# A transformer block's routing stage on one Trainium2 core: the picks in one comparison, the tokens formed in two halves later, a register load moved

## The reference, cut to what matters

```python
def moe(h, w_router, b_router, w_gate, b_gate, w_up, b_up, w_down, b_down):
    logits = h @ w_router + b_router
    top_logit, top_idx = lax.top_k(logits, TOP_K)      # 4 of 32 experts
    gates = jax.nn.softmax(top_logit, axis=-1)
    ...
        g = jnp.minimum(xb @ w_gate[e] + b_gate[e], 7.0)
        u = jnp.clip(xb @ w_up[e] + b_up[e], -7.0, 7.0)
        act = g * jax.nn.sigmoid(1.702 * g) * (u + 1)
        return act @ w_down[e] + b_down[e]
```

## Time and profile before

| | |
|---|---|
| median of 3 runs | 1881.03 us (1880.22 to 1882.22) |
| the profiled execution: its own time | 1879.11 us |
| its span, first to last instruction | 1877.3 us |
| mean granted TensorE clock | 0.996 |
| PE busy / DVE busy / ACT busy | 1824.7 / 505.1 / 348.3 us |
| router, from the scaled logits to the end of the block | 208.9 to about 221.6 us |
| experts' block, first gather to the last matmul of w_down | 221.9 to 1140.8 us |

### The profile page before, as it was taken

One profiled execution on the slowest core, in us unless ns is written; L12 is line 12 of the kernel. 1 busy time (PEld: TensorE's weight loads), 2 busy tenths in 40 slices (PEclk: granted clock), 3 DMA queues, 4 the chain that ended last, 5 costly groups with the idle time before them and its releaser, 6 DMA issues. The chain is left out here.

```text
span 1877.3 us, 21793 instructions
## 1 busy us (share of the span) xinstructions
PE 1824.7 (97%) x8661; PEld 998.6 (53%) x8662; DVE 505.1 (27%) x1093; ACT 348.3 (19%) x688; POOL 10.9 (1%) x14
## 2 busy tenths in 40 slices
PE   6999899999999999999999999999999999999998
PEld 5757533333333333333333336768885466788743
DVE  1754411111011111011111104542025443211355
ACT  3221411111111111111111113332000032220001
POOL 0000000000000000000000000000000000000001
PEclk9999899999999999999999999999999999999999
DMA  9986599999999999999999999423355443134252
GB/s 401 324 184 276 207 416 430 431 432 432 431 431 431 433 431 431 431 431 432 431 431 430 432 429 328 155 105 105 135 176 177 146 174 135 45 135 158 86 170 102
DMA packets 101218, 558.43 MB, mean 297 GB/s; under 512 B 16936, under 2 KB 33805, under 8 KB 74413
## 3 DMA queue, kind: packets, MB, share of 16 engines
q1 hardware_dynamic: 98612, 553.06, 72.4%
q10 hardware_dynamic: 2554, 4.63, 1.9%
HBM read 552.43 MB, written 5.23 MB: 297 GB/s over the span
## 5 line engine op out<-in xcount | busy, mean ns | idle before, releaser
L1362 PE MATMUL ps<-ring,xs 128*64 128x512 f32 x2112 | 466.9, 593 | 8.5 <-DMA ring<-in_w_up 4.7
L1362 PEld LDWEIGHTS ps<-ring,xs 128*64 128x64 f32 x2112 | 151.1, 137 | 312.7 <-issue 293.9
L1416 PE MATMUL ps<-ring,actT 128*64 128x512 f32 x1056 | 233.9, 595 | 0.0
L2149 PE MATMUL ps<-hT,ring 128*128 128x256 f32 x1024 | 222.0, 379 | 0.2 <-ACT hT L1614 0.2
L2149 PEld LDWEIGHTS ps<-hT,ring 128*128 128x128 f32 x1024 | 194.3, 190 | 27.0 <-ACT hT L1614 0.6
L2174 PE MATMUL ps<-ring 128*128 128x512 f32 x448 | 192.8, 592 | 0.0
L1416 PEld LDWEIGHTS ps<-ring,actT 128*64 128x64 f32 x1056 | 73.1, 137 | 158.5 <-issue 131.7
L1489 DVE TENSOR_SCALAR hT<-ps 128x512 f32<-128x512 f32 x33 | 22.8, 692 | 448.0 <-PE ps L1362 448.0
L2174 PEld LDWEIGHTS ps<-ring 128*128 128x128 f32 x448 | 85.0, 190 | 105.8 <-issue 105.7
L1937 PE MATMUL ps<-hT,ring 128*128 128x256 f32 x512 | 117.9, 383 | 4.3 <-ACT hT L1614 2.9
L1937 PEld LDWEIGHTS ps<-hT,ring 128*128 128x128 f32 x512 | 94.7, 190 | 23.2 <-issue 5.9
(11 more groups left out here) (434 smaller groups left out, 1548.1 us busy)
## 6 DMA issues: line engine op xcount, KB each, us to landing
ring<-in_w_up SPq DMA_DIRECT2D x64, 2048.0 KB, 23.2
ring<-in_w_down SPq DMA_DIRECT2D x64, 2048.0 KB, 24.2
ring<-in_w_gate SPq DMA_DIRECT2D x64, 2048.0 KB, 22.7
ring<-in_mlp_w SPq DMA_DIRECT2D x16, 2048.0 KB, 7.7
ring<-in_mlp_w SPq DMA_DIRECT2D x32, 1024.0 KB, 5.3
ring<-in_w_mod SPq DMA_DIRECT2D x8, 2048.0 KB, 15.4
ring<-in_odd_w_in SPq DMA_DIRECT2D x6, 2048.0 KB, 7.7
ring<-in_w_mod SPq DMA_DIRECT2D x8, 1024.0 KB, 14.1
```

Source lines behind the costliest of these rows:

```text
L1362: mm = pe.matmul(ps[SLOTS * half:SLOTS * (half + 1), bank, :], xs[:, c % 4, c // 4 * SLOTS:(c // 4 + 1) * SLOTS], weights(v, 8 * part + c) ...
L1416: mm = pe.matmul(ps[SLOTS * half:SLOTS * (half + 1), Y, :], actT[:, f % 4, f // 4 * SLOTS:(f // 4 + 1) * SLOTS], weights(v, 16 + f)[:, hal ...
L2149: mm = pe.matmul(ps[:, bank + f // 2, (f % 2) * SEQ:(f % 2 + 1) * SEQ], mlp_w1[layer][g % 2][:, c, f * P:(f + 1) * P], hT[:, c, :], start= ...
```

## The change

1. The masks: one `tensor_tensor` for each half of the tokens compares iota, repeated four times, with the four index columns, repeated 32 times (128x4x32, into a new tile `marks`); one `tensor_reduce` for each half adds over the four. Four instructions in place of eight.
2. The tokens: no longer between masks and gates. The first half is formed behind the integer table and ahead of the wait for the spread keys, the second behind the copy of the gates, as DVE's last instruction of the block.
3. PE: `begin` of banks 5, 6, 7 moves from before the spread (with its wait for both halves of the tokens) to behind it. Banks 4 and 5 are begun at once, 6 and 7 behind the first half of the tokens. The last filler is two matmuls instead of one.
4. SP's code is as it was; its wait for both halves of the tokens ahead of the last `load_ahead` now ends when the second half is formed.
5. Experts' block: PE's `passes(pe)` and its wait for b_down move ahead of the wait for `xrow_sb` and of the transposes.

```diff
@@ stage_first, tensor @@
             keep_busy(m, pe, 4, 4)
-            pe.wait_ge(picked, 8)
+            pe.wait_ge(picked, QT)
...
             pe.matmul(ps[0:1, 3, 0:PASSES], more[:, 3:4], pick, start=True, stop=True).then_inc(more_ps, 1)
-            pe.wait_ge(h2_ok, QT)
-            for b in (5, 6, 7):
-                begin(b)
             pe.wait_ge(turned_sb, 2)
             pe.wait_ge(more_chain, 10)
...
             pe.wait_ge(turned_sb, 4)
             begin(4)
-            keep_busy(m, pe, 0, 1)
+            begin(5)
+            pe.wait_ge(h2_ok, 1)
+            begin(6)
+            begin(7)
+            keep_busy(m, pe, 3, 2, SEQ)
             pe.wait_ge(m.brows_in, 32)
@@ stage_first, vector @@
-            for k in range(TOPK):
-                for i in range(QT):
-                    if k == 0:
-                        v.tensor_scalar(mask[:, i, :], iota[:, 0:EXPERTS], indexf[:, i, 0:1], None, ALU.is_equal).then_inc(picked, 1)
-                    else:
-                        v.wait_ge(picked, QT * (k - 1) + i + 1)
-                        v.scalar_tensor_tensor(mask[:, i, :], iota[:, 0:EXPERTS], indexf[:, i, k:k + 1], mask[:, i, :],
-                                               ALU.is_equal, ALU.add).then_inc(picked, 1)
-            v.wait_ge(h2_ps, 1)
+            hits = marks[:].rearrange("p (i k e) -> p i k e", i=QT, k=TOPK)
+            every = iota[:, 0:EXPERTS].rearrange("p (k e) -> p k e", k=1).to_broadcast([P, TOPK, EXPERTS])
             for i in range(QT):
-                b = (6, 0)[i]
-                v.scalar_tensor_tensor(h2[:, i, :], ps[:, b:b + 2, :].rearrange("p a n -> p (a n)"), stats[:, 18 + i:19 + i], shrow,
-                                       ALU.mult, ALU.add).then_inc(h2_ok, 1)
+                v.tensor_tensor(hits[:, i, :, :], every, spread(indexf[:, i, 0:TOPK], EXPERTS), ALU.is_equal).then_inc(hit, 1)
+            for i in range(QT):
+                v.wait_ge(hit, i + 1)
+                v.tensor_reduce(mask[:, i, :], hits[:, i, :, :].rearrange("p k e -> p e k"), AX, ALU.add).then_inc(picked, 1)
             v.wait_ge(exped, 2)
-            v.wait_ge(picked, 8)
+            v.wait_ge(picked, QT)
...
             v.tensor_scalar(m.table[:, PASSES + 1 + EXPERTS:], ps[0:1, 3, PASSES + 1:PASSES + 1 + EXPERTS], -1.0, None, ALU.add).then_inc(table_ok, 1)
+            def tokens_of(i):
+                b = (6, 0)[i]
+                v.scalar_tensor_tensor(h2[:, i, :], ps[:, b:b + 2, :].rearrange("p a n -> p (a n)"), stats[:, 18 + i:19 + i], shrow,
+                                       ALU.mult, ALU.add).then_inc(h2_ok, 1)
+            v.wait_ge(h2_ps, 1)
+            tokens_of(0)
             v.wait_ge(spread_ps, 1)
             v.tensor_copy(m.keys[:].rearrange("p i n -> p (i n)"), ps[:, 2, 0:2 * PASSES]).then_inc(spread_sb, 1)
...
             v.tensor_copy(m.gates[:].rearrange("p i n -> p (i n)"), ps[:, 2, 2 * PASSES:4 * PASSES]).then_inc(spread_sb, 1)
+            tokens_of(1)
@@ stage_experts, tensor @@
             gather()
             biases(((0, G), (1, U)))
+            n = passes(pe)
+            pe.wait_ge(bdown_in, 32)
             pe.wait_ge(xrow_sb, 1)
             turn_x()
             keep_busy(m, pe, Y, 1)
-            n = passes(pe)
-            pe.wait_ge(bdown_in, 32)
```

More of the change, by code:

```diff
@@ L339, in stage_first @@
     key = scratch((QT, EXPERTS))
+    marks = scratch((QT * TOPK * EXPERTS,))
     keyT = scratch((QT, P), EXPERTS)
@@ L346, in stage_first @@
     pick = m.pick[0:EXPERTS, :]
-    logit_sb, top8, top_i, top_f, picked, peak, exped, g_chain, rank_ps, key_ok, more_chain, more_ps, table_ok, turned_ps, turned_sb, spread_ps, spread_sb = (
-        m.sem(n) for n in ("logit_sb", "top8", "top_i", "top_f", "picked", "peak", "exped", "g_chain", "rank_ps", "key_ok", "more_chain",
+    logit_sb, top8, top_i, top_f, hit, picked, peak, exped, g_chain, rank_ps, key_ok, more_chain, more_ps, table_ok, turned_ps, turned_sb, spread_ps, spread_sb = (
+        m.sem(n) for n in ("logit_sb", "top8", "top_i", "top_f", "hit", "picked", "peak", "exped", "g_chain", "rank_ps", "key_ok", "more_chain",
                            "more_ps", "table_ok", "turned_ps", "turned_sb", "spread_ps", "spread_sb"))
```

## The result

The changed kernel takes 1882.75 us, median of 12 runs (1881.23 to 1885.18); the kernel before, timed beside it, 1879.89 us (12 runs, 1877.72 to 1882.22). The ratio is 1.0017, with a 95% interval of 1.0010 to 1.0025: about 3 us slower. The profiled execution of the changed kernel took 1883.17 us with a span of 1881.3 us, 4.0 us more than the 1877.3 before.

The account below looks back on a forecast made before the run. PE bounds the kernel, so the first pass's start decides. Gather 0.3 us later and register read 0.52 earlier, masks and loads 0, give -0.2: from the 1881.03 median to 1880.8 us; range 1877.9 to 1883.4.

Parts of the forecast that it names:

- rival 2: PE's new wait before the transposes: b_down lands behind w_down, after 226.8; time 1882.9 to 1884.7 us; chance 0.12.
- The loads: Late w_down load costs nothing alone; b_down sharing with it lands about 226.7, just before the transposes: 0 us.
- The router's terms: First block: L724 0.45 us earlier, spread 0.95 earlier, keys 1.15 earlier, but PE's fillers end it and gather starts 0.64 later.
- All of the router's gain is spent: End of first block: token halves, begins and filler use up the gain; gather starts at 222.5 against 221.86.
- The masks: Four mask instructions before the ranks: hidden behind PE's filler, 0 us; uncovered, worth -0.24 to +0.16 us.
- The register read: Moved ahead of the transposes, it brings the first pass 0.52 us nearer to them; bounds 0 and 1.25.
- Rival 3: Before the first pass: the read costs nothing, only the gather's delay of +0.3 us remains; 1881.3 us; chance 0.15.
- Rival 1: At the gather: more PE work raises the clock earlier, pass 1.8 to 2.8 us earlier; 1878.2 to 1880.7 us; chance 0.3.
- The rule on queues: Load queues: engines alternate between queues packet by packet, so b_down would land before w_down, making rival 2 void.

Follow-up runs that it names:

- run 4: Changed kernel with the experts' part as before (register read and b_down's wait behind the transposes); 1882.86 us, ratio 1.0022.
- run 5: Kernel before, with only SP's last load ahead (w_down) made to wait for DVE's copy of the gates; 1884.45 us, ratio 1.0028.
- run 1: Changed kernel with PE's wait for b_down back behind the transposes and filler, register read still ahead; 1883.67 us, ratio 1.0025.
- run 2: Changed kernel with SP's load of expert 0's first half of w_down moved behind b_down's landing; 1878.55 us, ratio 0.9996.
- run 3: Kernel before with only the experts' part of the change: register read and b_down's wait ahead of the transposes; 1878.48 us, ratio 0.9995.
- run 10: Kernel before with only the register read moved ahead of the transposes, b_down's wait left behind the filler; 1878.66 us, ratio 0.9994.
- run 6: Changed kernel with the w_down load split: three quarters issued early, only the last 512 KB waiting for the tokens' second half; 1878.14 us, ratio 0.9997.
- Run 12: The kernel of run 8 unchanged, timed a second time against the kernel before; 1877.08 us, ratio 0.9991.
- run 8: On top of run 2: token halves in DVE's idle stretches, begins of banks 6 and 7 in PE's wait for pick, one end filler; 1876.72 us, ratio 0.9987.

## Why the prediction was wrong

The forecast was -0.2 us; measured is 1.0017, slower, with the whole interval above 1. The time lies inside the range, but not by the forecast's mechanism. The ratio is that of rival 2 (1882.9 to 1884.7 of 1881.03, 1.0010 to 1.0020), its sign is in the trace (the transposes wait 2.32 us for b_down), and rival 2 is what happened.

**The loads, the failed step.** "b_down lands between 224.7 and 228.8 ... The middle, 226.7, is just ahead of 226.80: 0 in the sum." The bounds were from the right rows, but I took the middle between two rows that describe two different situations. An idle machine (1.9) did not apply, since the load was known to be in flight; the only row beside a stream was 6.0. Measured: 6.3 in the change, 6.7, 7.0 and 7.2 in runs 4, 5 and 1. By the nearer row the sum would have had 222.8 + 6.0 = 228.8 and rival 2's +1.9. A better picture was at hand too: w_down's own landing, 228.6 in my working, as the end that b_down shares. In the change the two ends are 230.8 and 231.0. The wait that the sum put at 0 was 2.3 us. Runs 2 and 5 show that the late load makes the loss: with w_down's load moved behind b_down the loss is gone, and with this load alone moved late, in the kernel before, it is there.

**What stands behind the wait.** Rival 2 began at +1.9 and reached +3.7 with a loss of clock, and the loss of clock is there: after PE's wait the first pass ran in part at half clock in the change and in runs 1, 4 and 5, and in none of the ten other traces. Runs 1 and 5 show that the old order would not have been spared either (+4.6 and +4.95 us between the medians), since the loop entries are queued behind the same wait: from the landing of b_down's second half to the pass there were 2.0 us in runs 1, 4 and 5, and the slow pass came on top.

**The router's terms** held in run 2, which has the change's router code and the clock of rows 7. L725 (L723 there) starts at 215.16 (215.20 forecast), the spread at 216.84 (216.95), the first half of the tokens at 217.56 (217.70), PE's fillers end the block and not DVE, and the gather starts at 222.19 (222.5). In the changed trace the agreement at L725, 215.26, is luck: the ranks began 0.6 us earlier than in rows 3, and the second filler took 2.63 us instead of 1.99 because the clock fell during it. Behind it the spread starts at 217.38 and the gather at 224.11, both later than forecast. "All of the router's gain is spent" was right: in run 2 the counts are taken 1.46 us earlier and the keys copied 1.3 us earlier than before, and the gather starts 0.3 us later.

**The masks** at 0 were right for the execution of rows 3; four instructions took 1.05 us (1.12 forecast). With the filler at full clock they are worth 0.31, a bit more than my bound of 0.24.

**The register read** was sized 0.52. Moving it took 0.77 us off in run 3, inside the bounds of 0 and 1.25, and 0.65 in the change; where the biases were slow the distance shrank by 1.10. So no run shows the read's own length. The Trainium skill, DMA: Bandwidth & Descriptors, "Latency and other measured facts", has a floor of about 600 ns for a tensor load; the trace does not contradict it and does not show it. Rival 3 is out as far as the traces go; the times of runs 3 and 10 alone could not be told from no change.

**Rival 1** did not occur in the changed trace: the gather took 3.63 us, at half clock, in spite of the second filler. It did occur in part in run 1, the same router code, where the gather took 2.80 us, and in run 5, with one filler, 2.85 us. So the clock can rise during the gather with one filler and with two; with b_down late this brings nothing.

**The rule on queues.** Against rival 2 I set the Trainium skill, DMA: Bandwidth & Descriptors, "Queues, rings and completion order": an engine takes turns between queues packet by packet. By it b_down would have landed before w_down; it landed behind it in the change and in runs 1, 4 and 5. The measurement decides. The packets of the change show where the rule does not describe this case: b_down's data did not start for 3.4 us, and moved beside w_down's only from then on. Why it started so late is open.

## What to carry to other kernels

When a step is moved, look at which transfers its semaphore releases, and what small transfer someone waits for at the new moment: here two token instructions moved within DVE's list pushed a 2 MB load onto a 128 KB one, and that cost 3 to 5 us. A small load that gates an engine should be issued ahead of the large one, or the large one split so that little is left in flight (runs 2 and 6). Work freed from a chain pays only if it goes where its engine was idle: with the two token instructions at the end of the block run 2 gained nothing that can be told. With them in DVE's gaps and one filler, two timings lie 1.8 and 2.8 us under before, at the edge of what can be told, and without the filler nothing is shown.

## What was not expected of the hardware

- A load of 2 x 64 KB on ACT's queue, issued 0.7 to 1.8 us behind one of 2 MB on SP's, landed only as that one did: its second half 0.2 us behind the large load in the change and in runs 1, 4 and 5, and 0.5 us behind the 512 KB of run 6. The medians of its two halves are 6.3 to 7.2 us after issue beside 2 MB, 2.5 beside 512 KB, 1.9 alone.
- The clock's fall to half came at different moments in executions of the same code. Run 12's program is run 8's: its filler behind the ranks took 3.65 us instead of 1.99, and its gather started at 221.46 instead of 219.63.
- A wait of PE ahead of the first pass (2.3 to 4.9 us idle) went with a half clock afterwards: the granted clock from 229 to 237 us was 0.79 in the change and in run 4, 0.65 in run 5 and 0.60 in run 1, and 1.00 in the kernel before. In run 5 this was about 3 us of the 6.4. That the wait makes the clock fall was not tested by itself.
- A DMA that lands late can show as "issue" (4.86 and 4.57 us in runs 1 and 5) when register work stands between the wait and the next matmul.
